# Rounded products of 512 moving columns, issued as two halves of 256

## What is computed

```python
def squared_relu_mlp(h, w_up, w_down):
    return jnp.square(jax.nn.relu(h @ w_up)) @ w_down
...
for layer in range(DEPTH):
    h = rms_norm(x, mix_norm[layer])
    ...
    x = x + squared_relu_mlp(rms_norm(x, mlp_norm[layer]), w_up[layer], w_down[layer])
...
for l in range(DEPTH):
    p = _rms_norm(x, norm_g[l]) @ w_in[l]
    ...
    x = x + m @ w_out[l]
```

## Time and profile before

| | |
|---|---|
| median of three runs | 2098.38 us |
| span of the profiled execution, first to last instruction | 2099.7 us |
| TensorE matmuls (PE) busy | 2076.6 us, 99%, 11148 instructions |
| TensorE weight loads (PEld) busy | 1645.5 us, 78%, 11148 instructions |
| VectorE, ScalarE, GpSimd busy | 947.6, 933.3, 759.2 us |
| bytes moved | 178.96 MB, 85 GB/s |

### The profile page before, as it was taken

The page is one execution under the profiler, slowest core; times in us unless marked ns, Lnnn a source line. Parts: engine busy times, 40 slices in busy tenths (PEclk is TensorE's granted clock), DMA queues, the critical chain, the costliest instruction groups (busy, mean ns, idle before and its releaser), DMA issues.

```text
span 2099.7 us, 28844 instructions
## 1 busy us (share of the span) xinstructions
PE 2076.6 (99%) x11148; PEld 1645.5 (78%) x11148; DVE 947.6 (45%) x1431; ACT 933.3 (44%) x1477; POOL 759.2 (36%) x316
## 2 busy tenths in 40 slices
PE   8999999999999999999999999999999999999999
PEld 5777788888888886668888888778788887877887
DVE  7875552112137256765211212667733354773331
ACT  7642453323236326774322324556742344765231
POOL 3332144444444630003444444344034443402443
PEclk9999999999999999999999999999999999999999
DMA  4442133333332431002333333232022333201232
GB/s 155 134 123 70 45 104 99 92 101 91 94 99 88 146 96 31 2 14 92 100 91 101 91 101 101 74 97 81 12 81 90 91 93 94 85 22 61 91 100 81
DMA packets 62710, 178.96 MB, mean 85 GB/s; under 512 B 17776, under 2 KB 18160, under 8 KB 62592
## 3 DMA queue, kind: packets, MB, share of 16 engines
q1 hardware_dynamic: 47600, 168.04, 26.3%
q10 hardware_dynamic: 14992, 9.22, 1.6%
HBM read 171.97 MB, written 3.70 MB: 84 GB/s over the span
## 4 chain that ended last, share of the span: by engine, by line
issue 48%; PE 34%; POOL 16%; ACT 1%; POOLq 0%; DMA 0%; SPq 0%; DVE 0%
POOL w_lo L2709 16%; PE banks L760 9%; PE banks L762 9%; PE banks L761 9%; PE banks L1282 1%; PE banks L1295 1%; PE banks L1267 1%; PE banks L811 1%; PE banks L1273 1%; PE banks L1239 0%; DMA x<-in_x 0%; PE banks L1330 0%; POOLq L2715 0%; POOLq L2717 0%; PE banks L1331 0%
## 5 line engine op out<-in xcount | busy, mean ns | idle before, releaser
L2709 POOL TENSOR_TENSOR w_lo<-raw,w_hi 128x1024 fp32r<-128x1024 f32 (+1 forms) x312 | 759.0, 2434 | 1322.8 <-ACT w_hi L1415 1322.7
L760 PE MATMUL banks<-h_lo,w_hi 128*128 128x512 f32 (+1 forms) x1408 | 567.0, 403 | 9.3 <-POOL w_lo L2709 9.3
L762 PE MATMUL banks<-h_hi,w_hi 128*128 128x512 f32 (+1 forms) x1408 | 554.7, 394 | 0.0
L761 PE MATMUL banks<-h_hi,w_lo 128*128 128x512 f32 (+1 forms) x1408 | 551.5, 392 | 0.0
L1415 ACT ACTIVATE w_hi<-raw 128x1024 fp32r<-128x1024 f32 (+1 forms) x312 | 327.9, 1051 | 489.4 <-PE banks L762 456.5
L760 PEld LDWEIGHTS banks<-h_lo,w_hi 128*128 128x128 f32 (+1 forms) x1408 | 264.4, 188 | 73.8 <-POOL w_lo L2709 8.7
L761 PEld LDWEIGHTS banks<-h_hi,w_lo 128*128 128x128 f32 (+1 forms) x1408 | 264.5, 188 | 62.2 <-issue 4.8
L762 PEld LDWEIGHTS banks<-h_hi,w_hi 128*128 128x128 f32 (+1 forms) x1408 | 264.3, 188 | 60.7 <-issue 0.7
L760 PE MATMUL banks<-a_lo,w_hi 128*128 128x512 f32 x768 | 304.5, 397 | 0.0
L762 PE MATMUL banks<-a_hi,w_hi 128*128 128x512 f32 x768 | 301.6, 393 | 0.0
L761 PE MATMUL banks<-a_hi,w_lo 128*128 128x512 f32 x768 | 299.8, 390 | 0.0
(11 more groups left out here) (365 smaller groups left out, 2466.5 us busy)
## 6 DMA issues: line engine op xcount, KB each, us to landing
raw<-in_weights SPq DMA_DIRECT2D x311, 512.0 KB, 3.6
x<-in_x SPq DMA_DIRECT2D x4, 512.0 KB, 6.2
AT<-row_dram ACTq DMA_DIRECT2D x4, 512.0 KB, 7.6
out<-x SPq DMA_DIRECT2D x8, 256.0 KB, 2.6
eg<-row_dram ACTq DMA_DIRECT2D x8, 128.0 KB, 3.3
phase<-in_phase ACTq DMA_DIRECT2D x1, 706.0 KB, 4.9
phase<-in_phase ACTq DMA_DIRECT2D x1, 704.0 KB, 4.2
ld_dram<-Ld ACTq DMA_DIRECT2D x1, 512.0 KB, 5.4
```

Of the source, the lines that this page charges most:

```text
L760: mm(out, w_hi, x_lo, start=first, stop=False)
L761: mm(out, w_lo, x_hi, start=False, stop=False)
L762: return mm(out, w_hi, x_hi, start=False, stop=last)
L2709: return nc.gpsimd.tensor_tensor(c.w_lo[:, slot, 0:n], c.raw[:, slot, 0:n], c.w_hi[:, slot, 0:n].bitcast(F32), ALU.subtract)
```

## The change

Each call of `three` issues six matmuls instead of three. The first half of the columns gets all three products, then the second half. The first product of the first half clears the bank; the last product of the second half closes the sum, and it is the instruction that carries the signal of the caller. The order within each element's sum stays the same. The same stationary operand stands on both sides of the border between the halves (`w_hi`), and is loaded again.

```diff
     def three(out, w_hi, w_lo, x_hi, x_lo, first, last):
 
-        mm(out, w_hi, x_lo, start=first, stop=False)
-        mm(out, w_lo, x_hi, start=False, stop=False)
-        return mm(out, w_hi, x_hi, start=False, stop=last)
+        for h in range(2):
+            half = slice(h * (T // 2), h * (T // 2) + T // 2)
+            mm(out[:, half], w_hi, x_lo[:, half], start=first and h == 0, stop=False, skip_group_check=True)
+            mm(out[:, half], w_lo, x_hi[:, half], start=False, stop=False, skip_group_check=True)
+            ins = mm(out[:, half], w_hi, x_hi[:, half], start=False, stop=last, skip_group_check=True)
+        return ins
```

## The result

The changed kernel takes **2122.73 us** (median of four runs, 2122.34 to 2125.22) against 2098.03 of the kernel before (four runs, 2094.12 to 2100.65) on the same chip: a ratio of 1.0127, interval 1.0113 to 1.0142. It is slower, as forecast; 2134 was 11 us too much. The profiled executions differ by 21.4 us of span.

A forecast was written before the change was run, and what follows sets the result against it. TensorE's row of instructions was taken as the bound. 14544 x (117 - 114.55) = 35.6 us more than the median of 2098.4 gave 2134 us, with a range of 2090 to 2214; the likeliest case alone has 2105 to 2170.

The forecast's parts named there:

- The bound: Whole kernel: TensorE, busy 2076.6 of 2099.7 us, sets the time; every other engine is busy under half of that.
- The removed and added instructions: Rounded products: 7272 matmuls of 512 columns and 7272 loads out, 14544 of 256 and 14544 loads in; issue costs nothing.
- The load costed at nothing: Weight load before each half: 112 ns fits within the 117 ns distance with 5 ns to spare, so it adds nothing.
- 117 ns at 256 columns: Start-to-start distance of each half, from the line 5 + 0.4375 x columns; against 114.55 it adds 35.6 us.
- the 115 to 119.5 that was asked of the MLP: Sign in the changed profile: an MLP distance outside 115 to 119.5 ns would make the prediction wrong.
- I take 229.1 ns for all.: All 7272 rounded matmuls of 512 columns given one start-to-start distance, 229.1 ns, 1666 us in sum.
- spread evenly over the MLP and projection stretches: Where the new time would appear; stages without rounded products, 800 to 900 us, would keep their length.
- A fixed start cost: Rival: all 15.8 ns beyond the columns belong to each stream's start, 122.5 ns per half, 2214 us; chance 0.18.
- The load lands late: Rival: late weight loads make each half 125 to 127 ns, 2250 to 2280 us; chance 0.06.
- The load is the bound, and that is faster: Rival: short streams lose little, loads alone set 112 ns per half, kernel gains 37 us, 2061 us; chance 0.12.
- No change: Rival: excess purely proportional to columns, distance per half between 114.1 and 115.0 ns; chance 0.11.
- The Trainium skill's rule of 2.5 ns beside the columns: Estimate for rounded matmuls: distance is columns / 2.4 plus about 2.5 ns, so the change costs 18 us, giving 2117.

The follow-up runs named there:

- quarters: Four matmuls of 128 columns for each product of 512 of the kernel before; 3864.39 us in one run.
- experiment 9: Kernel before, `h`, `a` moved down and `m`, `cn`, `d` up 64 bytes: 2081.14 us; or a 64-byte gap ahead of the weights instead: 2080.18 us.
- experiment 6: `h` and `a` moved down by 64 bytes: in the changed kernel 2166.41 us, ratio 1.0301; in the kernel before 2083.07 us, ratio 0.9904.

## Why the prediction was right, and where it was off

**The bound.** Right: TensorE's row is the span, no other engine's busy time moved, no new wait came.

**The removed and added instructions.** Right: 18420 matmuls, each with its load; no price of the issue shows, as 888 + 884 in 100 us had said; everything outside the rounded products changed by 0.2 us.

**The load costed at nothing.** Right. It was given 112 ns and measures 111.7 at full clock (quarters); both distances at 256 columns lie above it. Its cover is nearly gone, as the forecast said: 1.6 ns are left at 113.3.

**117 ns at 256 columns**, from the line through 75, 145 and 229. Right for two thirds of the products, 117.8 ns, within the 115 to 119.5 that was asked of the MLP. But the reason given, a slower rate per column with 5 ns at a start, is not what the runs show. At one placement the excess is a fixed 13.3 ns a matmul; at another two halves together pay 13.3 and the whole 20.0. Three points read at 10 ns, of two different operands, happened to lie on a line. That the line hit is luck, as far as the runs show: nothing measured why 320 and 160 columns of `kc` should speak for 256 of `h`.

**"I take 229.1 ns for all."** This is the step that failed. The two values were in the rows: `m` with 397 ns beside `a` with 388 (`a` itself has 388 between 1020 and 1320 us and 397 or 398 between 1600 and 1700), and 231.6 against 228.3 ns by stretch, which are 233.3 and 228.8 when starts are counted. The prediction gave the lower value to 2216 calls; it held for about 1600, since `h` and `a` of the late parts are at 233.3 like `m`. Nor do its own three figures give 229.1: weighted by calls they give 228.7. I averaged them and called the spread a detail of reading; they were two steady states, and the one with 233.3 answers to the split with a gain. The sum with four distances is 4800 x 6.7 - 1700 x 6.7 = 20.7 us, 22.4 with the other 770 products, against the 35.6 forecast, and 2098.4 + 22.4 = 2121 would have been within 2 us. The forecast's own total was within 11 us because the products that gained made up for a loss of 6.7 ns on the others that it had put at 4.9 (2 x 117 - 229.1). That the new time would be "spread evenly over the MLP and projection stretches" fell with it.

**The rivals.** *A fixed start cost* (0.18) is wrong for this kernel and exact for the one with `h` and `a` moved by 64 bytes: 120.0 is 106.7 + 13.3. What I read as evidence for it, the spread of 387 to 398 ns, follows the distances (388 ns where the next product starts after 226, 397 where it starts after 233), and at the placement of experiment 9 it is all but gone: 755 of the 768 rows of `a` at L761 have 389. *The load lands late* (0.06): nothing of it appears, not at 113.3 either. *The load is the bound, and that is faster* (0.12): its stream came down to 106.7 + 6.7 in some 1700 products, which is below its threshold of 114.1, without the load becoming the bound; had all products behaved so, 226.7 ns each, the kernel would have gained 4800 x 2.2 + 1700 x 6.7 = 22 us. *No change* (0.11) is excluded by the interval of the ratio; a quarter of the products gained as much each as two thirds lost, which is no balance. The Trainium skill's rule of 2.5 ns beside the columns ("Back-to-back issue gap"), which gave 2117 us, came within 6 us of the result for the wrong reason: measured are 6.7 to 13.3 ns at 256 columns, never 2.5, and the same page's sentence under "Step-by-step: what each phase is for", that loading the next weights takes no read bandwidth from the running matmul, doesn't explain why the place of the weights in relation to the moving operand changes the pace.

**What stays open.** What chooses between 228.9 and 233.3 (117.8 and 113.3) at unchanged addresses: `m` (experiment 9) excludes the operand's own place and the stage, and points to the products that ran ahead, but no run changed those alone, and what sets the first such run of the late parts is open. And whether the cause is that the load and the stream read SBUF at the same time. The latter is argued only: the relative address counts, and at 1.2 GHz no excess shows, neither at the start, where the loads have 40 columns, nor in the quarters with loads of 128 (213.3 ns, below). No kernel took the loads away, so it wasn't tried.

## What to carry to other kernels

Before a matmul is split, list its start-to-start distance by stage from stretches that hold whole runs of it, and treat two values that are 2% apart as two cases rather than as scatter: here a split lost in one and gained in the other. And where moving and stationary operand are both read without a pause, try their relative placement before their size: a gap of 64 bytes brought 1.0%, the best that any split brought was 0.5%. An offset is also a hidden variable in any comparison of two layouts.

## What the runs showed of the hardware

**The pace depends on the relative address** of the moving operand and the weights, by up to 6.7 ns in 233, and reverses the verdict on a split (table above).

**Two steady distances at one placement**, each of them kept through runs of 840 to 3072 matmuls. Neither the operand's own place nor the stage decides which: `m` at its unchanged place has 233.3 ns, or 229.0 where `h` and `a` are moved (experiment 9).

**The clock fell while TensorE had hardly a pause.** In the kernel of quarters, which streams 128 columns for each 112 ns load, matmuls stood 111.7 ns apart at full clock, but for one fall of 27 us at 1332 us, until 2455 us. The timeline where it turns:

```profile
2454.99 0.28 PE L763 MATMUL banks<-cn_hi,w_lo 128*128 128x128 f32 x1
2455.11 0.32 PE L764 MATMUL banks<-cn_hi,w_hi 128*128 128x128 f32 x1
2455.23 0.41 PE L762 MATMUL banks<-cn_lo,w_hi 128*128 128x128 f32 x1
2455.44 0.41 PE L763 MATMUL banks<-cn_hi,w_lo 128*128 128x128 f32 x1
```

From there they start 0.213 us apart, the granted clock being 0.50, which is the lower level of 1.2 GHz, until 2674 us, and again for most of 3220 to 3421; about 1800 matmuls in all, those at 1332 us among them, at 213 instead of 112 ns, 1800 x 0.1016 = 183 us. What the engine had done in the 30 us before each fall: mostly the same back-to-back quarters, with some matmuls of other kinds, and no pause of more than 13 ns; of each 112 ns the columns of a quarter stream for 53 (128 / 2.4). This is one run. The kernels of whole products and of halves had the granted clock at 1.00 in every stretch shown, but for short falls, such as 3.4 us at 202.5 us in the changed kernel and 10.2 us at 201.7 in the profiled execution of experiment 6's kernel of whole products, which took 2088.43 us where the median is 2083.07. So in the one run of quarters the lower clock was a second price beside the load; in the one of 384 and 128 columns it fell too, three times for 3.4 us.

**At the lower clock the load takes longer too.** With 0.50 granted, quarters follow each other at 213.3 ns, twice 106.7, though their columns need only 106.7 (128 / 1.2): the load is still the bound, and the 5 ns that it has above 106.7 at full clock are gone.
